# A hybrid retention, convolution and expert layer on one core: the written-out orders of four engines redone ahead of the gather stream

## The chip, the cores and the metric

The kernel runs on one core of a Trainium2 chip. The metric is the device time of one execution in microseconds. All arithmetic is float32. Five engines run their own instruction lists in parallel and meet at semaphores: PE (TensorE, matmuls and transposes), DVE (VectorE), ACT (ScalarE), POOL (GpSimd) and SP (SyncE, which here only issues DMAs). POOL also issues the indirect DMAs, called gathers below.

## What is computed

The reference runs one layer on 512 prompt frames and 32 frames of a running stream, 544 rows of 1024 numbers. Cut to what matters:

```python
h = rmsnorm(x, norm_mix)
q, k, v, g, a, b = split(h @ w_in)               # 4 x 512 for retention, 2 x 512 for the convolution
s_new, o = scan(retention_block, state, (rotary(q), rotary(k), v))   # 4 heads of 128
y_ret = silu(g) * group_norm(o)
c = depthwise_conv(concat(conv_buf, a * sigmoid(b)), taps=31) + bias
y_conv = silu(layer_norm(c))
x = x + concat(y_ret, y_conv) @ w_out
h2 = rmsnorm(x, norm_ffn)
for each of 8 heads:                             # product-key experts
    scores = two key halves of (h2 @ peer_query) against 128 keys each
    16 best sums of the two top-16 lists -> 16 experts of 16384, gate = softmax
    act = gelu(h2 . peer_down[expert]);  x = x + sum(gate * act * peer_up[expert])
return rmsnorm(x, norm_final), new states
```

## The kernel before

The 544 rows are cut in five tiles: 0 to 3 of 128 prompt rows, and tile 4 (`SAMPLE`) of 32 stream rows. The expert part is 34 "virtual tiles": head times prompt tile (32 of them), and two in which the 32 stream rows of four heads lie side by side. Each virtual tile needs 16 gathers. A gather fetches for each of 128 rows the line of one expert, `peer_down` beside `peer_up`, 8 KB a row and 1 MB in all. 544 gathers go through a ring of 12 slots in the tile `arena`. On each gathered slot DVE takes 128 dot products (`weigh`, L1329), ACT makes gelu, weight and a diagonal matrix of weights (`group`, L899 to L917), and PE adds the `peer_up` halves into PSUM by a matmul with this diagonal (`sum_up`, L1686). For the first eight gathers DVE does that sum (`sum_here`, L1339). When a slot has been used, POOL may gather into it again (`gathers`, L603).

The part ahead of the full stream is what the change touches. The same `arena` first holds the weights and the projections z = q, k, v, g of all tiles, so that the first gathers can only go out as z is used up. The steps and their names, with t the tile:

- `qkvg.s.t` (L1549, for the sample L1546): projection of section s (0 q, 1 k, 2 v, 3 g) on PE, 8 matmuls of 512 columns (16 records in the trace); ACT copies the result (`rows_in`).
- `ln_mean.b`, `ln_var.b` (L1558): channel sums of the convolution output on PE, b = 0 for the first 128 rows and 1 for the other 416. DVE subtracts the mean (`mean_off`), ACT squares (`squares`, L758) and takes the root (`root`, L763), DVE adds the squares and makes the inverse deviation (`square_sums`, `variance`, `inverse_deviation`, L1098 to L1122), then `conv_norm` (L1127, L1131), ACT `tanh`, DVE `conv_silu` (L1139). The whole convolution of 31 taps lies on DVE ahead of it and ends with L1220, which sets the semaphore `s_conv`.
- POOL turns q and k (`rotary`, L553 to L560) and weighs keys by decay (`decayed_keys`, L569).
- `head(t)` is `ret_qT.t` and `ret_kT.t`, four transposes each (L1508), copied by ACT (`turned_heads`, L735); `ret_scores.t` (L1575) and DVE's decay on it (L1151); `ret_out.t` (L1587, L1589); `ret_state.t` (L1596).
- `ret_out.t` is normed by head: DVE statistics (`ret_stats`, L1159), POOL `retention_root` (L574 to L578), ACT `head_norms` (L742), DVE times the gate (`ret_norm`, L1169), PE transposes it back (`ret_yT.t`), ACT copies (`turned_back`, L751). The gate comes from `gated` (L1078).
- `mix_out.t.i` (L1549 on `region_b`, for the sample L1546): output product, half i; DVE adds it to x (`mix_add`, L1195). ACT squares x (`mixed_squares`, L661), POOL takes the root (`mixed_root`), DVE norms (`peer_norm`, L1252), PE transposes (`ffn_t.t`), then `query.t` (L1620) and `scores.t` (L1633), copied by ACT (`first_query`, `first_scores`, L834).
- DVE searches the 16 best in three steps, `top_first`, `top_second`, `top_sums` (L1264 to L1314). The last line writes `expert`, the row numbers that the gathers of this virtual tile read.

No scheduler decides any order. PE runs through `plan()`; the other engines run through calls written out one by one, and two lists, `EMPTY_ORDER`, state in which order DVE and ACT empty the PSUM banks. PE's jobs take the eight banks in turn, and a wait is a comparison with the number of jobs done:

```python
JOB = {name: n for n, name in enumerate(JOBS)}
BANK = {name: n % BANKS if n < FIRST_SUM else ...}
def filled(name):
    act.wait_ge(s_pe, JOB[name] + 1)
```

So the engines that read a job wait for all PE jobs ahead of it too. POOL's first gathers wait for more than their expert numbers (shortened):

```python
pool.wait_ge(s_idx, 1)
gathers(0, 0, 1)
retention_root(2)
gathers(0, 2, 4)
gathers(0, 6, 10)                                  # each waits for sum_here to free its slot
pool.wait_ge(s_pe, JOB[("ret_yT", 4)] + 1)
gathers(0, 15, TOPK)
pool.wait_ge(s_pe, JOB[("mix_out", SAMPLE, 0)] + 1)
gathers(1, 0, 2)
```

Of the kernel before, what the change touches and what calls it, by code (L numbers as in the profile page):

```python
# [118 lines left out]
def plan():  # L119

    def rows(s, *tiles):
        return [("qkvg", s, t) for t in tiles]
# [4 lines left out]
    def scores(t):  # L127
        return [("ret_scores", t)]
# [68 lines left out]
ln_mean.0 ln_mean.1 ln_var.0 ln_var.1 ret_scores.0 ret_state.0 mix_out.0.0 mix_out.0.1 ret_scores.1 ret_state.1  # L197
ret_scores.2 mix_out.1.0 mix_out.1.1 ret_state.2 ret_scores.3 mix_out.2.0 ret_state.3 mix_out.2.1 ret_scores.4
mix_out.3.0 mix_out.3.1 mix_out.4.0 mix_out.4.1 ret_state.4
# [4 lines left out]
qkvg.3.1 qkvg.3.2 qkvg.3.4 ret_yT.0 ret_qT.1 ret_kT.1 qkvg.3.3 ffn_t.0.0 ffn_t.0.1 ret_qT.2 ret_kT.2 ret_out.1 query.0  # L204
scores.0 ret_yT.1 ret_out.2 ret_qT.3 ret_kT.3 ret_yT.2 ffn_t.1.0 ffn_t.1.1 ret_out.3 ret_qT.4 ret_kT.4 query.1
ret_yT.3 scores.1 ret_out.4 ret_yT.4 ffn_t.2.0 ffn_t.2.1 query.2 scores.2 ffn_t.3.0 ffn_t.3.1 ffn_t.4.0 ffn_t.4.1
# [30 lines left out]
def build(nc, x_prompt, x_sample, x_turned, state_ret, conv_state, weights, head_weights, params, consts, gain_ffn, gain_final,  # L237
          experts, y_prompt, y_sample, ret_prompt, ret_sample, conv_prompt, conv_sample):
    ctx = ExitStack()
    with ctx:  # L240
# [280 lines left out]
        def _(pool):  # L521
# [64 lines left out]
            rotary(2)  # L586
            rotary(3)
            retention_root(0)
# [32 lines left out]
            gathers(0, 2, 4)  # L621
            pool.wait_ge(s_pe, JOB[("ret_yT", 1)] + 1)
# [3 lines left out]
            mixed_root(1)  # L626
            decayed_keys(3)
# [31 lines left out]
        def _(act):  # L659
# [137 lines left out]
            turned_back(0)  # L797
            turned_heads(1)
            rows_in(S_G, 3)
# [140 lines left out]
            normalized(0)  # L940
            head_norms(2)
            turned_heads(3)
            mixed_squares(1)
            turned_back(2)
            turned_rows(1)
            group(0, 0)
            head_norms(3)
            turned_heads(4)
            first_query(1)
            turned_back(3)  # L950
            first_scores(1)
# [6 lines left out]
            turned_rows(2)  # L958
            mixed_squares(3)
            mixed_squares(SAMPLE)  # L960
            normalized(1)
            first_query(2)
            group(0, 2)
            first_scores(2)
            turned_rows(3)
            group(0, 3)
            turned_rows(4)
            group(1, 0)
            first_query(3)
# [10 lines left out]
            later_query(1, 1)  # L980
            group(2, 1)
            later_query(1, 2)
            later_query(1, 3)
            group(2, 2)
            later_scores(1)
# [31 lines left out]
        def _(dve):  # L1017
# [367 lines left out]
            gate_scales(0)  # L1385
            mix_add(1, 1)
            ret_norm(2)
            ret_state(2)
            ret_scores(3)
            dve.wait_ge(s_gain, 16)  # L1390
            peer_norm(1)
            weigh(0, 0)
            mix_add(2, 0)
            ret_stats(3)
# [429 lines left out]
```

## Time and profile before

| what | value |
|---|---|
| median of 3 runs | 1663.01 us (1662.77 to 1663.81) |
| the profiled execution, its own time | 1664.46 us |
| its span | 1662.7 us |
| busy: PE, DVE, ACT, POOL | 83%, 71%, 34%, 43% |
| moved by DMA | 608.39 MB, 570.46 of them by the gathers |
| mean granted TensorE clock | 0.946 of full speed |

A row of a timeline is: start in us from the span's start, length in us, engine, line of the kernel, operation, out<-in with shapes, x count. In brackets behind it stands how long the engine was idle before, and what released it. A row of the windows is: stretch, its length, busy us of PE, weight loads (PEld), DVE, ACT and POOL with the number of instructions, then the granted clock of PE (1.00 is 2.4 GHz, 0.50 is 1.2 GHz), the mean busy share of the 16 DMA engines, and GB/s. Matmul ends are modelled, so neighbouring rows of PE overlap by some 0.15 us.

### The profile page before, as it was taken

How to read it: one execution, taken by the hardware profiler on the slowest of the kernel's cores; microseconds unless marked ns; L12 is line 12 of the kernel's file. 1: busy time of each engine (PE TensorE's matmuls, PEld its weight loads, DVE VectorE, ACT ScalarE, POOL GpSimd, SP SyncE). 2: the span in 40 equal slices, each digit the busy share in tenths (PEclk: the TensorE clock that was granted, in tenths of full speed). 3: DMA queues.
4: the chain of work that ended last, by engine and by line, in shares of the span. 5: the costliest groups of instructions: out<-in, count | busy, mean ns of one | idle time of the engine just before them, and what ended most of it. 6: DMA issues, size and time to landing. Idle time of an engine off the chain costs nothing.

```text
span 1662.7 us, 14018 instructions
## 1 busy us (share of the span) xinstructions
PE 1383.8 (83%) x4311; PEld 678.6 (41%) x4311; DVE 1174.9 (71%) x2555; ACT 573.3 (34%) x1785; POOL 716.7 (43%) x633
## 2 busy tenths in 40 slices
PE   7999999998898789778977897789779877777733
PEld 6744465554353335324433443344324423332311
DVE  3997758966876777677767776777777777676755
ACT  3112231632433333333333333333433333333342
POOL 0004624644444445444444444445444444444552
PEclk9999999999899999999999999999999999999955
DMA  7203227999999999999999999999999999999996
GB/s 293 102 1 100 110 77 279 371 421 422 422 420 422 421 422 420 422 421 422 420 422 421 422 421 422 421 421 421 421 422 421 421 422 420 419 420 421 414 421 256
DMA packets 87978, 608.39 MB, mean 366 GB/s; under 512 B 11104, under 2 KB 13664, under 8 KB 16224
## 3 DMA queue, kind: packets, MB, share of 16 engines
q0 software_dynamic: 78336, 570.46, 82.9%
q1 hardware_dynamic: 9568, 37.04, 5.9%
q8 instruction: 34, 0.56, 0.1%
q14 instruction: 40, 0.33, 0.1%
HBM read 604.19 MB, written 2.88 MB: 365 GB/s over the span
## 4 chain that ended last, share of the span: by engine, by line
DMA 44%; PE 37%; DVE 10%; issue 3%; ACT 3%; POOL 2%; DVEq 0%; SPq 0%; POOLq 0%
DMA arena<-experts,expert 44%; PE ps L1686 18%; PE ps L1549 8%; PE ps L1649 5%; DVE arena L1329 4%; PE ps L1529 4%; POOL arena L603 2%; ACT weight L907 1%; ACT late L917 1%; PE ps L1508 1%; DVE cst L1305 0%; DVE cst L1308 0%; DVE picked L1312 0%; PE ps L1620 0%; ACT gl L899 0%
## 5 line engine op out<-in xcount | busy, mean ns | idle before, releaser
L1686 PE MATMUL ps<-arena,late 128*128 128x512 f32 x2016 | 950.3, 624 | 206.0 <-ACT late L917 205.7
L603 POOL DMA_INDIRECT arena<-experts,expert x544 | 645.2, 1186 | 732.4 <-PE ps L1686 627.5
L1329 DVE CUSTOM_DVE_ANT_0 arena<-arena,hn 128x1024 f32<-128x1024 f32 x544 | 656.7, 1222 | 384.9 <-DMA arena<-experts,expert 381.8
L1686 PEld LDWEIGHTS ps<-arena,late 128*128 128x128 f32 x2016 | 387.3, 198 | 745.0 <-issue 450.7
L899 ACT ACTIVATE gl<-dots 128x2 f32<-128x2 f32 (+1 forms) x274 | 55.8, 204 | 814.3 <-DVE dots L1329 814.3
L917 ACT ACTIVATE late<-cst,weight 128x128 f32<-128x128 f32 (+1 forms) x536 | 183.5, 389 | 8.8
L907 ACT ACTIVATE weight<-gl,gate 128x1 f32<-128x1 f32 x544 | 130.7, 287 | 8.9
L1549 PE MATMUL ps<-arena,hT 128*128 128x512 f32 x256 | 112.3, 598 | 0.0
L1649 PE MATMUL ps<-hT,region_b 128*128 128x272 f32 x448 | 106.9, 392 | 0.0
L1649 PEld LDWEIGHTS ps<-hT,region_b 128*128 128x128 f32 x448 | 85.1, 190 | 27.9 <-issue 12.4
L1072 DVE SCALAR_TENSOR_TENSOR region_b<-region_b,par 128x574 f32<-128x574 f32 x120 | 92.5, 813 | 4.5
L1549 PEld LDWEIGHTS ps<-arena,hT 128*128 128x128 f32 x256 | 48.7, 192 | 58.9 <-issue 58.8
L1680 PE MATMUL ps<-arena,late 128*32 128x256 f32 x256 | 29.7, 604 | 45.4 <-ACT late L917 45.4
L553 POOL TENSOR_TENSOR rot_tmp<-arena,cst 128x512 f32<-128x512 f32 (+1 forms) x5 | 6.3, 1265 | 124.8 <-DVE hn L1220 124.5
L1549 PE MATMUL ps<-arena,region_b 128*128 128x512 f32 x128 | 56.5, 595 | 2.5 <-issue 2.5
L1329 DVE DVE_READ_ACCUMULATOR2_ANT dots<- 128x1 f32 x544 | 44.6, 82 | 0.0
L873 ACT ACT_TABLE_LOAD x33 | 42.3, 1283 | 0.6
L899 ACT ACT_TABLE_LOAD x32 | 41.1, 1283 | 0.6
L1348 DVE TENSOR_TENSOR xs<-ps,xs 128x1024 f32<-128x1024 f32 x32 | 39.0, 1219 | 0.0
L1529 PE MATMUL ps<-hn,arena 128*128 128x272 f32 x160 | 36.8, 392 | 0.0
L1549 PEld LDWEIGHTS ps<-arena,region_b 128*128 128x128 f32 x128 | 23.8, 190 | 31.0 <-issue 30.9
L1680 PEld LDWEIGHTS ps<-arena,late 128*32 128x32 f32 x256 | 8.9, 150 | 66.1 <-ACT late L917 58.1
(174 smaller groups left out, 872.1 us busy)
## 6 DMA issues: line engine op xcount, KB each, us to landing
arena<-weights SPq DMA_DIRECT2D x6, 2048.0 KB, 11.0
region_b<-head_weights SPq DMA_DIRECT2D x8, 1152.0 KB, 9.5
arena<-experts,expert POOLq DMA_INDIRECT x544, 22.4
hT<-x_turned SPq DMA_DIRECT2D x2, 1088.0 KB, 7.2
arena<-weights SPq DMA_DIRECT2D x4, 512.0 KB, 10.7
xs<-x_prompt SPq DMA_DIRECT2D x4, 512.0 KB, 10.0
arena<-weights SPq DMA_DIRECT2D x2, 1024.0 KB, 13.9
y_prompt<-xs SPq DMA_DIRECT2D x4, 512.0 KB, 3.8
```

The source lines that it names most:

```text
L603: pool.indirect_dma_start(rows_of(n), None, experts, bass.IndirectOffsetOnAxis(ap=expert[:, vt % BUFS, k:k + 1], axis=0))\
L873: nc.scalar.activation(gate[:, u, :], best_s[:, u, :], ACT.Exp, bias=neg_max[:, u:u + 1], accum_out=gate_sum[:, u:u + 1]).then_inc(s_exp, 1)
L899: nc.scalar.activation(gl[:, vt % 2, ks], dots[:, vt % 2, ks], ACT.Gelu_apprx_tanh).then_inc(s_gelu, 1)
L907: ready = nc.scalar.activation(weight[:, vt % 2, k:k + 1], gl[:, vt % 2, k:k + 1], ACT.Copy, scale=gate[:, vt % BUFS, k:k + 1])
L917: nc.scalar.activation(diag[:, n % DIAGS, 0:base.shape[-1]], base, ACT.Copy, scale=weight[:, vt % 2, k:k + 1])\
L1072: return v.scalar_tensor_tensor(out=conv[:, c, :], in0=u[:, c, j:j + WIDE], scalar=gain, in1=conv[:, c, :], op0=ALU.mult, op1=ALU.add)
L1329: last = v.tensor_tensor_reduce(out=rows_of(n)[:, 0:D], in0=rows_of(n)[:, 0:D], in1=hn[:, tile_of(vt)], scale=1.0, scalar=0.0, op0=ALU.mul ...
L1348: v.tensor_tensor(out=xs[:, tile], in0=total, in1=xs[:, tile], op=ALU.add).then_inc(s_acc, 1)
L1529: last = mm(out[:, 0:HALF], w[:, c, k, :], columns[:, k, i * HALF:(i + 1) * HALF], start=k == 0, stop=k == KD - 1)
L1549: last = mm(out, lhs[:, k, lo:lo + r], w[:, k, :], start=k == 0, stop=k == KD - 1)
L1649: last = mm(ps[:, Q_BANKS + i, 0:HALF], weights[:, k, s * KEYS:(s + 1) * KEYS], hT[:, k, half * HALF:(half + 1) * HALF], start=k == 0, sto ...
L1686: last = mm(ps[:, 2 * (vt % 2) + half, :], diag[:, n % DIAGS, :], rows_of(n)[:, D + half * SEC:D + (half + 1) * SEC], start=k == first * G ...
```

## The change

Nothing is computed differently, and no size changes. On PE, DVE, ACT and POOL the steps named above change places, from the last k rows to virtual tile 3. SP's list is the same. The core of the diff:

```diff
@@ plan()
-    order += rows(S_Q, 2) + rows(S_K, 1) + rows(S_Q, 3) + rows(S_V, 3) + rows(S_K, 2)
-    order += [("ln_mean", 0)] + rows(S_Q, SAMPLE) + head(0) + [("ln_mean", 1), ("ln_var", 0)] + rows(S_K, 3)
-    order += [("ln_var", 1)] + scores(0) + rows(S_G, 0) + [("ret_out", 0)] + rows(S_G, 1) + [("ret_state", 0)]
-    order += rows(S_G, 2, SAMPLE) + back(0) + head(1) + rows(S_G, 3) + mix(0, 0) + mix(0, 1) + scores(1)
-    order += [("ret_out", 1)] + turn("ffn_t", 0) + [("ret_state", 1)] + head(2) + query(0) + back(1) + scores(2)
-    order += keys(0) + mix(1, 0) + [("ret_out", 2)] + mix(1, 1) + head(3) + [("ret_state", 2)] + back(2) + scores(3)
-    order += mix(2, 0) + turn("ffn_t", 1) + out(3) + head(4) + mix(2, 1) + query(1) + back(3) + scores(4) + keys(1)
-    order += mix(3, 0) + [("ret_out", 4)] + mix(3, 1) + [("ret_state", 4)] + back(4) + mix(4, 0) + mix(4, 1)
+    order += rows(S_Q, 2) + rows(S_V, 3) + rows(S_Q, 3) + rows(S_K, 1) + [("ln_mean", 0)] + rows(S_K, 2)
+    order += rows(S_Q, SAMPLE) + head(0) + [("ln_var", 0)] + [("ln_mean", 1)] + rows(S_K, 3) + scores(0)
+    order += [("ln_var", 1)] + rows(S_G, 0) + rows(S_G, 1) + [("ret_out", 0)] + rows(S_G, 2, SAMPLE)
+    order += [("ret_state", 0)] + back(0) + rows(S_G, 3) + mix(0, 0) + mix(0, 1) + head(1) + head(2) + scores(1)
+    order += [("ret_out", 1)] + turn("ffn_t", 0) + [("ret_state", 1)] + query(0) + back(1) + keys(0) + scores(2)
+    order += mix(1, 0) + [("ret_out", 2)] + mix(1, 1) + head(3) + [("ret_state", 2)] + back(2) + scores(3) + mix(2, 0)
+    order += out(3) + head(4) + turn("ffn_t", 1) + mix(2, 1) + query(1) + back(3) + keys(1) + scores(4)
+    order += [("ret_out", 4)] + mix(3, 0) + mix(3, 1) + [("ret_state", 4)] + back(4) + mix(4, 0) + mix(4, 1)
@@ gpsimd
             rotary(2)
+            retention_root(0)
             rotary(3)
-            retention_root(0)
...
             gathers(0, 2, 4)
+            decayed_keys(3)
+            mixed_root(1)
             pool.wait_ge(s_pe, JOB[("ret_yT", 1)] + 1)
             gathers(0, 4, 5)
             pool.wait_ge(s_pe, JOB[("ret_yT", 2)] + 1)
             gathers(0, 5, 6)
-            mixed_root(1)
-            decayed_keys(3)
@@ scalar
             squares(0)
             rows_in(S_Q, SAMPLE)
+            root(0)
+            squares(1)
             turned_heads(0)
-            squares(1)
-            root(0)
+            root(1)
             rows_in(S_K, 3)
-            root(1)
             rows_in(S_G, 0)
+            head_norms(0)
             tanh(0)
-            head_norms(0)
...
             turned_back(0)
+            rows_in(S_G, 3)
             turned_heads(1)
-            rows_in(S_G, 3)
...
             first_query(0)
+            turned_back(1)
             act.wait_ge(s_yconv, len(BLOCKS))
             first_scores(0)
-            turned_back(1)
@@ vector
             inverse_deviation(0)
+            ret_scores(0)
             variance(1)
-            ret_scores(0)
             inverse_deviation(1)
+            conv_norm(0)
+            conv_norm(1)
             gated(0)
             ret_stats(0)
-            conv_norm(0)
-            conv_norm(1)
             ret_norm(0)
             conv_silu(0)
+            ret_state(0)
             gated(1)
+            mix_add(0, 0)
+            gated(2)
             conv_silu(1)
-            gated(2)
-            ret_state(0)
             gated(SAMPLE)
+            mix_add(0, 1)
             gated(3)
-            mix_add(0, 0)
-            mix_add(0, 1)
             ret_scores(1)
```

The other hunks move, on DVE and ACT, the gate of virtual tile 0, head copies, dots, searches and PSUM sums of virtual tiles 0 to 3 by one or two places each, and on PE `sum_up(2, 0)` behind two of the query products of head 1. The two lists of `EMPTY_ORDER` follow these orders.

Three places show what moves. PE's list at the last k rows (L1549 is a projection, 40 or 48 matmuls are five or six of them; L1558 on `hn` is `ln_mean.0`; L1546 is the sample's q, and L1508 behind it head 0):

```order
 L1546 MATMUL ps<-arena,hT 32x128 x64
-L1549 MATMUL ps<-arena,hT 128x512 x48
+L1549 MATMUL ps<-arena,hT 128x512 x40
 L1558 MATMUL ps<-hn,ones_cw 128x128
+L1549 MATMUL ps<-arena,hT 128x512 x8
 L1546 MATMUL ps<-arena,hT 32x128 x32
 L1508 MATMUL ps<-cst,arena 128x128 x8
```

The channel mean moved ahead of the last of six projections, `qkvg.1.2`.

DVE's list behind the inverse deviation of the 416 rows (L1078 is the gate of tile 0, L1159 and L1162 are `ret_stats(0)`, L1127 and L1131 `conv_norm`, L1169 is `ret_norm(0)`), the counterpart of POOL's `retention_root(0)`, which the diff shows ahead of `rotary(3)`:

```order
-L1078 SCALAR_TENSOR_TENSOR arena<-late,arena 128x512
-L1159 BN_STATS bn<-ps 128x6 x4
-L1162 BN_AGGR mv<-bn 128x2 x4
 L1127 TENSOR_TENSOR region_b<-region_b,var 128x4x128
 L1131 TENSOR_SCALAR region_b<-region_b,half_ln 128x128 x4
 L1127 TENSOR_TENSOR region_b<-region_b,var 128x4x416
 L1131 TENSOR_SCALAR region_b<-region_b,half_ln 128x416 x4
+L1078 SCALAR_TENSOR_TENSOR arena<-late,arena 128x512
+L1159 BN_STATS bn<-ps 128x6 x4
+L1162 BN_AGGR mv<-bn 128x2 x4
 L1169 TENSOR_TENSOR hn<-hn,arena 128x512
```

The gate and the statistics of tile 0 moved behind both calls of `conv_norm`.

PE's list at the sample's retention (L1575 is `ret_scores.4`, L1633 `scores.1`, L1549 `mix_out.3.0`, L1587 with L1589 `ret_out.4`):

```order
 L1508 MATMUL ps<-cst,hn 128x128 x4
+L1633 MATMUL ps<-region_b,late 128x128 x2
 L1575 MATMUL ps<-hn 32x32 x4
-L1633 MATMUL ps<-region_b,late 128x128 x2
-L1549 MATMUL ps<-arena,region_b 128x512 x8
 L1587 MATMUL ps<-arena,hn 32x128
 L1589 MATMUL ps<-state,hn 32x128
```

The product `mix_out.3.0` no longer stands between the sample's scores and its `ret_out.4`; it comes behind.

## Rows read from the trace of the kernel before

**Rows 1.** the page: its length, and the queue of the gathers

```profile
span 1662.7 us, 14018 instructions
...
q0 software_dynamic: 78336, 570.46, 82.9%
```

**Rows 2.** windows: busy us (x instructions) by engine, PEclk, DMA share, GB/s

```profile
257.00:267.00 10.00, 10.00 (x53) 6.49 (x52) 7.64 (x18) 4.07 (x14) 5.94 (x7) 1.00 0.01 5
...
293.00:300.00 7.00, 6.26 (x141) 5.76 (x131) 5.96 (x18) 6.81 (x15) 4.71 (x6) 1.00 0.91 298
300.00:1641.00 1341.00, 1094.91 (x2884) 505.84 (x2886) 941.28 (x2154) 491.27 (x1586) 630.93 (x537) 0.94 1.01 420
```

**Rows 3.** timeline of POOL, four gathers: start, length, line, [idle before, releaser]

```profile
238.31 1.22 POOL L603 DMA_INDIRECT arena<-experts,expert  x1 [13.55 <-DVE expert L1314]
...
264.37 2.11 POOL L603 DMA_INDIRECT arena<-experts,expert  x1 [0.17 <-DVE xs L1339]
...
291.71 1.09 POOL L603 DMA_INDIRECT arena<-experts,expert  x1 [4.93 <-PE ps L1508]
...
295.14 1.34 POOL L603 DMA_INDIRECT arena<-experts,expert  x1 [0.88 <-PE ps L1546]
```

**Rows 4.** timeline of PE, K rows to the mixing products: its stalls

```profile
154.04 1.06 PE L1508 MATMUL ps<-cst,arena 128*128 128x128 f32 x8 [2.03 <-issue]
...
192.21 0.66 PE L1508 MATMUL ps<-cst,hn 128*128 128x128 f32 x4 [2.94 <-DVE hn L1169]
...
194.06 8.24 PE L1549 MATMUL ps<-arena,hT 128*128 128x512 f32 x16
...
218.01 0.49 PE L1587 MATMUL ps<-arena,hn 128*128 128x128 f32 x2 [1.09 <-DVE hn L1151]
...
230.13 7.11 PE L1549 MATMUL ps<-arena,region_b 128*128 128x512 f32 x16 [1.61 <-issue]
...
249.62 7.11 PE L1549 MATMUL ps<-arena,region_b 128*128 128x512 f32 x16 [0.63 <-issue]
...
273.24 7.11 PE L1549 MATMUL ps<-arena,region_b 128*128 128x512 f32 x16 [0.27 <-issue]
```

**Rows 5.** timeline of PE, and windows of 1 us, behind a stall of 3 us

```profile
349.06 8.83 PE L1686 MATMUL ps<-arena,late 128*128 128x512 f32 x16 [2.98 <-ACT late L917]
...
351.00:352.00 1.00, 1.00 (x3) 0.48 (x2) 0.93 (x4) 0.59 (x2) 0.00 (x0) 0.50 1.01 421
```

**Rows 6.** timeline of DVE: work beside busy POOL, and beside idle POOL (144.21)

```profile
144.21 0.76 DVE L1218 TENSOR_TENSOR hn<-region_b 128x574 f32<-128x574 f32 x1
...
173.38 1.50 DVE L1116 TENSOR_TENSOR region_b<-region_b 128x416 f32<-128x416 f32 x1
...
186.00 5.56 DVE L1131 TENSOR_SCALAR region_b<-region_b,half_ln 128x416 f32<-128x416 f32 x4
```

**Rows 7.** timeline of DVE, of ACT and of POOL

```profile
145.04 0.76 DVE L1220 TENSOR_TENSOR hn<-hn 128x574 f32<-128x574 f32 x1
...
181.03 0.88 DVE L1159 BATCH_NORM_STATS2 bn<-ps 128x6 f32<-128x128 f32 x4
...
191.48 0.68 DVE L1169 TENSOR_TENSOR hn<-hn,arena 128x512 f32<-128x512 f32 x1
...
150.96 0.63 ACT L758 ACTIVATE region_b<-region_b 128x512 f32<-128x512 f32 x1 [0.42 <-DVE region_b L1090]
...
186.08 1.51 ACT L742 ACTIVATE hn<-ps,rstd,ret_rstd 128x128 f32<-128x128 f32 x4 [1.29 <-POOL rstd L578]
...
221.87 0.23 POOL L574 TENSOR_SCALAR rstd<-mv 128x4 f32<-128x4 f32 x1 [3.02 <-DVE mv L1162]
...
223.56 0.20 POOL L578 TENSOR_TENSOR rstd<-rstd,ret_rstd 128x4 f32<-128x4 f32 x1
```

**Rows 8.** timeline of DVE: sums of tile 0, and dots behind gather 7

```profile
261.45 5.44 DVE L1339 SCALAR_TENSOR_TENSOR xs<-arena,weight,xs 128x1024 f32<-128x1024 f32 x4
...
274.62 1.22 DVE L1329 CUSTOM_DVE_ANT_0 arena<-arena,hn 128x1024 f32<-128x1024 f32 x1 [2.50 <-DMA arena<-experts,expert]
```

More of the change, by code:

```diff
@@ L196 @@
 EMPTY_ORDER = {"dve": named("""
-ln_mean.0 ln_mean.1 ln_var.0 ln_var.1 ret_scores.0 ret_state.0 mix_out.0.0 mix_out.0.1 ret_scores.1 ret_state.1
+ln_mean.0 ln_mean.1 ln_var.0 ret_scores.0 ln_var.1 ret_state.0 mix_out.0.0 mix_out.0.1 ret_scores.1 ret_state.1
 ret_scores.2 mix_out.1.0 mix_out.1.1 ret_state.2 ret_scores.3 mix_out.2.0 ret_state.3 mix_out.2.1 ret_scores.4
-mix_out.3.0 mix_out.3.1 mix_out.4.0 mix_out.4.1 ret_state.4
+mix_out.3.0 mix_out.3.1 mix_out.4.0 ret_state.4 mix_out.4.1
 """), "act": named("""
@@ L203 @@
 qkvg.1.4 qkvg.1.0 qkvg.0.2 qkvg.1.1 qkvg.0.3 qkvg.2.3 qkvg.1.2 qkvg.0.4 ret_qT.0 ret_kT.0 qkvg.1.3 qkvg.3.0 ret_out.0
-qkvg.3.1 qkvg.3.2 qkvg.3.4 ret_yT.0 ret_qT.1 ret_kT.1 qkvg.3.3 ffn_t.0.0 ffn_t.0.1 ret_qT.2 ret_kT.2 ret_out.1 query.0
-scores.0 ret_yT.1 ret_out.2 ret_qT.3 ret_kT.3 ret_yT.2 ffn_t.1.0 ffn_t.1.1 ret_out.3 ret_qT.4 ret_kT.4 query.1
-ret_yT.3 scores.1 ret_out.4 ret_yT.4 ffn_t.2.0 ffn_t.2.1 query.2 scores.2 ffn_t.3.0 ffn_t.3.1 ffn_t.4.0 ffn_t.4.1
+qkvg.3.1 qkvg.3.2 qkvg.3.4 ret_yT.0 qkvg.3.3 ret_qT.1 ret_kT.1 ffn_t.0.0 ffn_t.0.1 ret_qT.2 ret_kT.2 ret_out.1 query.0
+ret_yT.1 scores.0 ret_out.2 ret_qT.3 ret_kT.3 ret_yT.2 ret_qT.4 ret_kT.4 ffn_t.1.0 ffn_t.1.1 ret_out.3 query.1
+scores.1 ret_yT.3 ret_out.4 ret_yT.4 ffn_t.2.0 ffn_t.2.1 query.2 scores.2 ffn_t.3.0 ffn_t.3.1 ffn_t.4.0 ffn_t.4.1
 query.3 scores.3 scores.4
@@ L934, in _ @@
             first_query(0)
+            turned_back(1)
             act.wait_ge(s_yconv, len(BLOCKS))
             first_scores(0)
-            turned_back(1)
             softmax(0)
             gelu_next()
-            normalized(0)
             head_norms(2)
             turned_heads(3)
+            turned_back(2)
             mixed_squares(1)
-            turned_back(2)
+            turned_heads(4)
+            normalized(0)
+            group(0, 0)
             turned_rows(1)
-            group(0, 0)
             head_norms(3)
-            turned_heads(4)
             first_query(1)
+            first_scores(1)
             turned_back(3)
-            first_scores(1)
             group(0, 1)
@@ L958, in _ @@
             turned_rows(2)
+            normalized(1)
             mixed_squares(3)
             mixed_squares(SAMPLE)
-            normalized(1)
+            group(0, 2)
             first_query(2)
-            group(0, 2)
             first_scores(2)
+            group(0, 3)
             turned_rows(3)
-            group(0, 3)
+            group(1, 0)
             turned_rows(4)
-            group(1, 0)
-            first_query(3)
             softmax(2)
@@ L972, in _ @@
             normalized(2)
+            first_query(3)
             group(1, 2)
@@ L980, in _ @@
             later_query(1, 1)
+            later_query(1, 2)
             group(2, 1)
-            later_query(1, 2)
             later_query(1, 3)
+            later_scores(1)
             group(2, 2)
-            later_scores(1)
             normalized(3)
@@ L1385, in _ @@
             gate_scales(0)
+            ret_norm(2)
             mix_add(1, 1)
-            ret_norm(2)
             ret_state(2)
             ret_scores(3)
+            weigh(0, 0)
             dve.wait_ge(s_gain, 16)
             peer_norm(1)
-            weigh(0, 0)
+            ret_stats(3)
             mix_add(2, 0)
-            ret_stats(3)
             ret_state(3)
@@ L1402, in _ @@
             sum_here(1)
+            mix_add(3, 0)
             ret_stats(SAMPLE)
             top_second(1)
-            mix_add(3, 0)
             ret_norm(SAMPLE)
@@ L1408, in _ @@
             mix_add(3, 1)
+            mix_add(SAMPLE, 0)
+            gate_scales(1)
             peer_norm(2)
-            mix_add(SAMPLE, 0)
+            ret_state(SAMPLE)
             mix_add(SAMPLE, 1)
-            gate_scales(1)
-            ret_state(SAMPLE)
             weigh(0, 2)
@@ L1417, in _ @@
             weigh(0, 3)
+            weigh(1, 0)
             top_first(2)
-            weigh(1, 0)
             top_second(2)
             top_sums(2)
-            add(0)
+            gate_scales(2)
             weigh(1, 1)
-            gate_scales(2)
             weigh(1, 2)
             top_first(3)
+            add(0)
             top_second(3)
+            top_sums(3)
             weigh(1, 3)
-            top_sums(3)
             weigh(2, 0)
             gate_scales(3)
-            add(1)
             weigh(2, 1)
             weigh(2, 2)
-            weigh(2, 3)
+            add(1)
             top_first(4)
-            weigh(3, 0)
             top_second(4)
             top_sums(4)
+            weigh(2, 3)
+            weigh(3, 0)
             weigh(3, 1)
@@ L1442, in _ @@
             top_first(5)
+            top_second(5)
+            top_sums(5)
             weigh(3, 2)
-            top_second(5)
             weigh(3, 3)
-            top_sums(5)
             for vt in range(4, VT - 2):
@@ L1737, in _ @@
                     sum_up(step[1], step[2])
+            sum_up(2, 0)
             later_query(1, 0)
             later_query(1, 1)
-            sum_up(2, 0)
             later_query(1, 2)
```

## Prediction

> **What bounds the kernel now.** Read the page first, its length and its queues [rows 1]: one queue, the gathers, moves 570 MB in a span of 1662.7 us and takes 82.9% of all 16 DMA engines' time. Then the windows [rows 2]. They say when the stream is full for good: from 300 to 1641 us the DMA share is 1.01 at 420 GB/s, and before that it has a hole from 257 to 267 (share 0.01) and is short again from 293 to 300 (0.91). So 1341 us of the span are bytes over a rate, and an order of instructions changes neither. What an order can change is when the stream becomes unbroken. The timeline of POOL [rows 3] names what each gather waited for. The first (238.31) waited for the expert numbers from VectorE, the seventh (264.37) for a weighted sum that frees a slot, the sixteenth (291.71) for a transpose on PE (`ret_yT.4`), the seventeenth (295.14) for the product `mix_out.4.0` on PE. From the sixteenth on the queue is never empty long enough to matter. Hence the rule for this change: the end moves by as much as gathers 15 and 16 (numbered from 0) move, and these hang on the end of PE's list before the full stream. An earlier first gather alone only makes the hole behind it wider.
>
> PE does the same matmuls before and after, so its end moves by the difference of its stalls and slow stretches. The timeline of PE [rows 4] has those of before between the last K rows and `mix_out.3.1`: 2.03, 2.94, 1.09, 1.61, 0.63 and 0.27 us, together 8.6. One product took 8.24 instead of 7.11 us behind the stall of 2.94 (1.1 more). Smaller pieces, without a row, I put at 0.6. Sum 10.3 us.
>
> **The change, part by part.**
>
> *Mean before K rows.* `ln_mean.0` now stands ahead of `qkvg.1.2`. It needs the channel sum that VectorE ends at 145.04 + 0.76 = 145.8 [rows 7]. PE gets there at 142.9: head 0 came at 154.04 after a stall of 2.03 [rows 4], so PE was done at 152.0, and the sample product and one product of 7 us lie ahead of that. PE now stalls 2.9 us, and the stall of 2.03 goes. A stall of that length lowers the granted clock in this trace: behind 2.98 us idle the window at 351 shows 0.50 (1.2 GHz), and the 16 records took 8.83 us where 7.11 is usual [rows 5, 4]. Price 1.7 us; bounds 0 (behind 2.03 us nothing slowed) and 1.7; I take 1.7, as 2.9 is nearer to 2.98. ScalarE's `squares(0)` still stands behind the copy of those K rows, so it leaves 150.96 [rows 7] for about 155.5: the early mean brings nothing, and `ln_var.0`, which PE now asks for ahead of `ln_mean.1`, comes 0.9 us late.
>
> *VectorE without POOL.* `retention_root(0)` moves ahead of `rotary(3)` on POOL, and on VectorE `ret_stats(0)`, which it waits for, moves behind both `conv_norm`. POOL's list thus stops at about 171.8, with `rotary(2)`, until `ret_stats(0)`. Queued behind it are `rotary(3)`, `rotary(4)`, `decayed_keys(1)`; the first needs them at `ret_kT.3` near 242 and ends near 205, so nobody waits. VectorE then works alone. Beside a busy POOL a 416-column operation took 1.50 us and four of them 5.56; beside an idle POOL one of 574 columns took 0.76 [rows 6]. So 416 columns alone cost 0.6 (estimate by columns), bounds 0.6 and 1.5. Four such in `inverse_deviation(1)` and four in `conv_norm(1)` save 8 x 0.9 = 7.2 us. The reciprocal of the same width I leave as it is, since no row shows it shorter. Against it: the late squares, and the root ahead of `squares(1)`, cost the chain 4 us. And three things now follow `conv_norm(1)` in a row: the statistics (0.88, and some 0.3 for their sums), POOL's root (221.87 to 223.76, 1.9) and `head_norms(0)` (1.5) [rows 7], together 4.6 us, of which the statistics' 1.2 lay on the chain before too. The gate of tile 0, beside an idle POOL, takes 0.9 less. `ret_norm(0)` ended at 192.2 [rows 7] and comes at 192.2 - 7.2 + 4 + 4.6 - 1.2 - 0.9 = 191.5. PE, with K rows late and both G products ahead of `ret_out.0`, asks for it at 192.5, 1 us later. The stall of 2.94 goes, and the 1.1 of slow clock with it.
>
> The Trainium skill ("SBUF — State Buffer", Who interferes with whom) says that VectorE and GpSimd share one port pair as an exclusive lock, that two SBUF inputs or a 2-port mode need it, and that other one-input operations do not. By this rule the multiplications shorten and the reciprocal does not, as in the sum; rows 6 agree (1.50 against 0.76).
>
> *Heads 1 and 2 behind the mixing products.* 1.8 us of transposes move; no work is added. `mix_out.0.1` then ends about 2 us earlier. `ret_out.1` still waits for `ret_scores(1)`: 0.6 in place of 1.09. Head 2 no longer stands between the rows of tile 0 and `query.0`. ScalarE has `turned_back(1)` ahead of `first_scores(0)`, so `mix_out.1.0` does not wait (1.61 goes), while the search gets its scores 1 us later than it could. The first gather goes out about 1.9 us earlier, at 236.4. Ahead of `mix_out.2.0` 0.2 in place of 0.63.
>
> *`ret_out.4` ahead of `mix_out.3.0`.* It needs `ret_scores(4)`, which VectorE has behind `weigh(0, 1)`, and that waited 2.50 us for gather 7 until 274.62 [rows 8]. Gather 6 leaves when the sum of tile 0 (261.45, rows 8) has freed its slot; head 4 and the sums come 4.5 us earlier, and the POOL piece behind them too, so gather 6 goes out 5.4 us earlier (264.37 to about 259) and gather 7 lands at 269.2. `weigh(0, 1)` and `ret_scores(4)` end at 270.9, PE is there at 268.8: a new stall of 2.0, where the product of 7 us covered it before. The 0.27 goes.
>
> The sum of stalls after: 2.9 + 1.7 + 0.9 + 0.6 + 0.2 + 2.0 = 8.3 us against 10.3: PE ends its list **2.0 us** earlier, gathers 15 and 16 go out at 289.7 and 293.1, and the stream becomes whole 2.0 us sooner. Behind it nothing counts: dots, searches, sums and projections of tiles 1 to 3 change places under a queue that is full [rows 2]. The profiled execution took 1664.46 us for a span of 1662.7, 1.45 above the median of 1663.01; less 2.0 it is 1662.5, and the median 1661.0. A measurement of this kernel tells about 0.2% (3.3 us) from no change.
>
> **The rivals.** (a) *The clock holds.* If PE keeps 2.4 GHz through the stall of 2.9, as it did through 2.03, and the stall at `ret_out.4` is gone because gather 7 lands in time, it is 1661.0 - 1.7 = 1659.3 for the first and 1657.3 for both. For it: 2.9 is at the edge. Against: rows 5, and the same happened behind 2.94.
> (b) *The clock falls twice.* The new stall of 2.0 to 2.5 follows the small matmuls of scores 1 and head 4; with 1.7 more it is 1662.7. For it: a stall of 2.94 behind such small work was enough [rows 4]. The Trainium skill ("TensorE: Matmul & The Clock Gate", Part 4) holds that transposes do not count as busy in the way that matmuls do, which speaks for it, as this stretch has them; rows 4 have 2.03 us idle with no slow product behind, which speaks against.
> (c) *Slower: VectorE is not freed.* If the 1.50 us is the operation's own length, `ret_norm(0)` comes 7.2 us later, at 198.7. It decides from 192.5 on, when PE wants it: PE stalls 6.2 us before `ret_yT.0`, and the clock falls once more (1.7). 1661.0 + 6.2 + 1.7 = 1668.9. For it: no row shows a 416-column operation beside an idle POOL. Against: 574 columns in 0.76.
> (d) *The stream ignores it.* If gathers 15 and 16 had slack the end would stay at 1663.0. Against: the queue was short of work just there (share 0.91 from 293 to 300, rows 2).
>
> **How the numbers follow.** Forecast 0.38; (a) 0.34; (b) and (d) 0.12; (c) 0.11; the rest 0.05. The range 1656.5 to 1666.0 holds the forecast, (a), (b), (d) and part of the way to (c); the forecast's own is 1659.5 to 1662.5. Faster than 1659.7 is (a) with the forecast's lower edge, 0.37; slower than 1666.3 is (c) and some of the rest, 0.13; within 0.2% 0.50.
>
> **What would show it.** Step one: PE idle near 143 for 3 us, PEclk at 0.5 behind it, `squares(0)` near 155. Step two: no POOL row between 172 and 186, 416-column rows near 0.6 us, no stall before `ret_yT.0`. Step three: first gather near 236.4, `mix_out.1.0` without a stall. Step four: PE waiting for VectorE's `ret_scores(4)` near 269 for about 2 us. The end: gathers 15 and 16 near 289.7 and 293.1. It is wrong if the span moves otherwise than these two do, or if the DMA share falls below 1 anywhere between 300 and 1641.

## The result, and the profile after

| what | before | the change |
|---|---|---|
| median | 1663.55 us (14 runs) | 1667.22 us (14 runs, 1666.29 to 1670.88) |
| ratio | | 1.0025, 95% interval 1.0016 to 1.0033 |
| the profiled execution, its span | 1664.46, 1662.7 us | 1667.13, 1665.3 us |
| mean granted TensorE clock | 0.946 | 0.944 |

The change is slower, by 3.7 us. The forecast was 1661.0, and its range ended at 1666.0. A sentence of the section on the change has to be read the right way round: on PE, `sum_up(2, 0)` moves from *behind* the first two query products of head 1 to *ahead* of them, so that all four products now stand in one row, with `sum_up(2, 1)` behind them.

The windows of after, with the columns of [rows 2], and four stretches more. The rows at 273, 288, 388 and 394 were not shown of before: there the clock is 1.00 in all four, and the shares at 288, 388 and 394 are 1.00, 1.01 and 1.00.

```profile
257.00:267.00 10.00, 10.00 (x45) 6.17 (x45) 9.05 (x14) 3.96 (x14) 7.20 (x9) 1.00 0.59 214
273.00:274.00 1.00, 1.00 (x5) 0.36 (x4) 1.00 (x2) 0.00 (x0) 0.00 (x0) 0.50 0.99 418
...
288.00:293.00 5.00, 4.69 (x17) 2.24 (x15) 4.73 (x15) 0.27 (x2) 0.02 (x1) 1.00 0.10 41
293.00:300.00 7.00, 4.99 (x136) 4.32 (x136) 5.00 (x17) 5.98 (x15) 4.78 (x6) 1.00 0.71 226
300.00:1641.00 1341.00, 1097.16 (x2892) 509.77 (x2892) 940.94 (x2154) 491.24 (x1585) 641.65 (x538) 0.94 1.01 420
...
388.00:394.00 6.00, 6.00 (x15) 2.66 (x14) 0.00 (x0) 0.00 (x0) 2.82 (x3) 1.00 0.76 277
394.00:400.00 6.00, 4.53 (x26) 3.26 (x25) 3.83 (x18) 4.04 (x14) 0.94 (x1) 1.00 0.98 367
```

The hole from 257 to 267 is half filled, as gather 6 goes out earlier. A new one stands from 288 to 293, and one more at 388, inside the stream that [rows 2] showed as full. The long window hides it: two or three us in 1341 round away in a share of 1.01. That is the first thing to learn here, since the forecast rested on that long window.

POOL of after, the same gathers as [rows 3]: the first, number 6, 15 and 16, then the two on either side of the hole at 388.

```profile
237.46 1.22 POOL L603 DMA_INDIRECT arena<-experts,expert  x1 [13.48 <-DVE expert L1314]
...
259.65 2.06 POOL L603 DMA_INDIRECT arena<-experts,expert  x1 [0.22 <-DVE xs L1339]
...
292.98 1.06 POOL L603 DMA_INDIRECT arena<-experts,expert  x1 [5.78 <-PE ps L1508]
...
296.42 1.02 POOL L603 DMA_INDIRECT arena<-experts,expert  x1 [0.89 <-PE ps L1546]
...
373.08 1.14 POOL L603 DMA_INDIRECT arena<-experts,expert  x1 [0.78 <-PE ps L1686]
389.96 0.94 POOL L603 DMA_INDIRECT arena<-experts,expert  x1 [15.74 <-PE ps L1686]
```

PE of after, its timeline at the places of [rows 4]: the channel sums, the transposes of tile 0, the mixing products of tiles 1 and 2, the retention output of the stream rows and what follows it, and the sums behind the searches that [rows 5] showed.

```profile
146.37 0.79 PE L1558 MATMUL ps<-hn,ones_cw 128*128 128x128 f32 x2 [2.81 <-DVE hn L1220]
...
192.52 0.60 PE L1508 MATMUL ps<-cst,hn 128*128 128x128 f32 x4
...
271.54 0.40 PE L1587 MATMUL ps<-arena,hn 32*32 32x128 f32 x2 [1.59 <-DVE hn L1151]
...
273.09 0.63 PE L1587 MATMUL ps<-arena,hn 32*32 32x128 f32 x2
...
275.35 16.00 PE L1549 MATMUL ps<-arena,region_b 128*128 128x512 f32 x32
...
356.34 16.46 PE L1686 MATMUL ps<-arena,late 128*128 128x512 f32 x32 [6.04 <-ACT late L917]
372.64 14.83 PE L1649 MATMUL ps<-hT,region_b 128*128 128x272 f32 x64
387.31 7.03 PE L1686 MATMUL ps<-arena,late 128*128 128x512 f32 x16
```

VectorE of before, then of after, at the first dot product of `weigh(1, 3)`:

```profile
345.45 1.22 DVE L1329 CUSTOM_DVE_ANT_0 arena<-arena,hn 128x1024 f32<-128x1024 f32 x1
```

```profile
352.74 1.22 DVE L1329 CUSTOM_DVE_ANT_0 arena<-arena,hn 128x1024 f32<-128x1024 f32 x1
```

So there are two losses, and they are read in this order. **At 271.54** PE waits 1.59 us, and from 272.6 to 279.4 it runs at half clock (the window at 273 shows 0.50): the small products of `ret_out.4` take 3.8 us in place of 2.67, and the 32 mixing records 16.00 in place of 13.9, together 3.2 us. Gather 15 goes out at 292.98, 1.3 us *later* than before. **At 356.34** PE waits 6.04 us for scaled copies where it waited 2.98 [rows 5], because VectorE's dots `weigh(1, 3)` begin at 352.74 and not at 345.45. The sums that free the slot for the gather at 389.96 (number 48) start at 387.31, not at 379.26; before, that gather left at 381.92. The last packet of the gather ahead of it ended at 390.3 before and ends at 391.5 after. So before the queue still had 8.4 us of work when this gather was issued, and after it has 1.6: the queue runs dry.

The DMA packets say what each costs. The table gives, in us against before, when the last packet of a gather of queue 0 ended (gathers numbered from 0; 144 packets each, in the order in which they ended), for this profile and for those of the experiments below.

| gather | change | kernel 1 | kernel 2 | kernel 3 | kernel 4 | kernel 7 | kernel 8 |
|---|---|---|---|---|---|---|---|
| 15 | +1.6 | +0.8 | +0.9 | -2.2 | -1.8 | -1.6 | -5.6 |
| 30 | +0.2 | -0.3 | +2.1 | -2.4 | -2.5 | -2.3 | -6.1 |
| 46 | +0.3 | -0.3 | +2.1 | -2.4 | -2.6 | -2.3 | -6.1 |
| 96 | +2.9 | -0.3 | +5.0 | +2.2 | -2.6 | +1.7 | -6.1 |
| 528 | +2.4 | -0.4 | +4.8 | +1.8 | -2.2 | +1.3 | -6.0 |

Between 46 and 96 lies the dry stretch, 2.7 to 4.7 us where there is one. In kernels 2, 3 and 7 it has a second, shorter part: from 412 to 420 their shares are 0.94, 0.94 and 0.92, where the change and kernel 4 have 1.02 and 1.00.

Between 15 and 30 a profile can gain or lose a us or more by itself. Kernel 2 has PE's code of before up to there and shows +2.1. Its PE at `mix_out.4.0`, below that of before:

```profile
292.38 3.76 PE L1546 MATMUL ps<-arena,region_b 128*32 128x128 f32 x128 [0.96 <-issue]
```

```profile
292.75 5.37 PE L1546 MATMUL ps<-arena,region_b 128*32 128x128 f32 x128 [0.96 <-issue]
```

Behind the same wait of 0.96 us the clock fell in one profile (0.50 from 293 to 296) and held in the other (1.00). So one profile can't give the price of the start of the stream; for that the medians of the runs are used.

### The profile page after: what moved, and what is told of

Read it like the earlier page. It is cut to its first block, busy times and chain, and to the rows that moved or that the text cites. A ratio compares the mean times of both kernels' runs of the same rounds, so it can differ in the third digit from the quotient of the medians.

```text
span 1665.3 us, 14018 instructions
## 1 busy us (share of the span) xinstructions
PE 1388.1 (83%) x4311; PEld 682.0 (41%) x4311; DVE 1163.4 (70%) x2555; ACT 571.3 (34%) x1785; POOL 724.4 (43%) x633
## 4 chain that ended last, share of the span: by engine, by line
DMA 41%; PE 35%; DVE 13%; issue 4%; DVEq 3%; ACT 2%; POOL 2%; SPq 0%; POOLq 0%; ACTq 0%
DMA arena<-experts,expert 41%; PE ps L1686 20%; PE ps L1549 6%; PE ps L1649 5%; DVE arena L1329 4%; DVE region_b L1072 3%; DVEq L1213 3%; PE ps L1529 2%; POOL arena L603 2%; ACT weight L907 1%; ACT late L917 1%; DVE cst L1305 1%; DVE cst L1308 1%; DVE picked L1312 1%; DVE best_i L1271 0%
## 5 line engine op out<-in xcount | busy, mean ns | idle before, releaser
L603 POOL DMA_INDIRECT arena<-experts,expert x544 | 657.3, 1208 | 722.2 <-PE ps L1686 606.3
L1549 PE MATMUL ps<-arena,hT 128*128 128x512 f32 x256 | 112.5, 598 | 0.0
L1549 PEld LDWEIGHTS ps<-arena,hT 128*128 128x128 f32 x256 | 49.0, 193 | 59.7 <-issue 59.4
L1549 PE MATMUL ps<-arena,region_b 128*128 128x512 f32 x128 | 58.2, 611 | 0.4 <-issue 0.4
L1549 PEld LDWEIGHTS ps<-arena,region_b 128*128 128x128 f32 x128 | 24.7, 197 | 30.5 <-issue 30.4
```

Of the source, the lines that this page charges most:

```text
L603: pool.indirect_dma_start(rows_of(n), None, experts, bass.IndirectOffsetOnAxis(ap=expert[:, vt % BUFS, k:k + 1], axis=0))\
L1549: last = mm(out, lhs[:, k, lo:lo + r], w[:, k, :], start=k == 0, stop=k == KD - 1)
```

## The experiments

Two theories stood at first. Theory E: the early stall and clock fall at `ret_out.4` cost the time. Theory L: the late order does, through the dry stretch. Each kernel ran 11 or 12 times beside 33 or 35 runs of before. The interval of a ratio is 0.0009 to either side, which is 1.5 us; a difference of two medians is no surer than that. The kernels are numbered as they ran.

**1. The late part undone.** The change, with this taken back (VectorE's dots and searches from `weigh(1, 0)` on, two ScalarE copies and PE's sums):

```diff
-            top_first(3)
-            add(0)
-            top_second(3)
-            top_sums(3)
-            weigh(1, 3)
+            add(0)
...
+            top_first(3)
+            top_second(3)
+            weigh(1, 3)
+            top_sums(3)
...
-            sum_up(2, 0)
             later_query(1, 0)
             later_query(1, 1)
+            sum_up(2, 0)
```

> The changed kernel with the late part of the change alone undone (TensorE: sums (2,0) again between the first and the last two query products of head 1; ScalarE: the scaled copies (2,1) and (2,2) again ahead of a query copy and the score copies; VectorE: dots and searches of tiles 1 to 3 in the old order). Theory L (the late order lets the full stream run dry once near 390 us): about 3 us faster than the change, 1664.2 us, and no hole in the transfers near 388 to 400 us. Theory E (the stall and the second clock fall near 270 us, which delay gathers 15 and 16 by 1.3 us, cost the time): 1667.2 us, within 0.5 of the change.

Measured: 1665.56 us, ratio 1.0012 (1.0003 to 1.002), 1.7 us better than the change (2.2 by the ratios). The share from 388 to 394 is 1.02. The hole is gone, but not all of the loss: the time lies between what theories L and E had.

**2. The late part alone**, the same hunks put into the kernel before.

> The kernel before with only that late part of the change put in. Theory L: about 3 us slower than before, 1666.5 us, with a hole in the transfers near 385 to 400 us though everything up to 330 us is as before. Theory E: 1663.5 us, as before.

Measured: 1666.85 us, ratio 1.0019 (1.001 to 1.0028): 3.2 us slower than before, with 15.95 us of idle POOL ahead of the same gather and a share of 0.93 from 388 to 394. The late part by itself makes a slow kernel. That settles theory L as one half. The profile's own time, 1669.68 us, is 2.8 above the median and has the clock fall at 293 in it.

**3. The retention output back behind its cover.**

```diff
-    order += [("ret_out", 4)] + mix(3, 0) + mix(3, 1) + [("ret_state", 4)] + back(4) + mix(4, 0) + mix(4, 1)
+    order += mix(3, 0) + [("ret_out", 4)] + mix(3, 1) + [("ret_state", 4)] + back(4) + mix(4, 0) + mix(4, 1)
```

> The changed kernel with the retention output of the sample tile behind the first half of mix 3 on TensorE again, all else as in the change. Both theories expect no stall near 270 us and no second clock fall, and gathers 15 and 16 some 3 us earlier (near 290 and 293 us). Theory E: the time falls by 1.3 to 3.3 us, to 1664 to 1666. Theory L: the stream is held at its dry stretch near 390 us, which stays where it was, so 1667.2 us, within 0.7.

Measured: 1665.06 us, ratio 1.0006 (0.9997 to 1.0014), 2.2 us better than the change (3.2 by the ratios). PE and POOL of this kernel:

```profile
271.23 7.11 PE L1549 MATMUL ps<-arena,region_b 128*128 128x512 f32 x16 [1.18 <-issue]
278.27 0.40 PE L1587 MATMUL ps<-arena,hn 32*32 32x128 f32 x2
...
289.70 1.06 POOL L603 DMA_INDIRECT arena<-experts,expert  x1 [6.58 <-PE ps L1508]
293.13 1.02 POOL L603 DMA_INDIRECT arena<-experts,expert  x1 [0.89 <-PE ps L1546]
```

No clock fall, and gathers 15 and 16 at 289.70 and 293.13: what the forecast had, 289.7 and 293.1. But the table shows that of the 2.4 us that the stream is ahead at gather 46 nothing is left at gather 96 (this profile, 1666.39 us, is 1.3 above the kernel's median). Theory L had no gain here and was off by 2 us; theory E had 1664 to 1666, which holds. Both hold in part, so they were joined.

**4. Both undone.**

> Both undone at once: the retention output of the sample tile behind the first half of mix 3, and the late part in the old order. Theory L: 1664.2 us if the start of the full stream is absorbed by the slack near 312 to 320 us as in the kernel before, down to 1660.9 if it is not (gathers 15 and 16 then come 1.9 us earlier than before the change). Theory E alone: as the third kernel of this call, 1664 to 1666.

Measured: 1662.09 us, ratio 0.9986 (0.9978 to 0.9995). 5.1 us better than the change, a little more than the two gains apart (1.7 and 2.2). That would fit one limit hiding behind the other, but the excess is within the uncertainty. With these two places mended the rest of the change is a gain of 1.5 us on before (2.3 by the ratio), near the 2.0 of the forecast.

**5 to 7. Which piece of the late part?** Kernel 4, with one engine's piece put back in each time: PE's, ScalarE's, VectorE's.

> The fourth kernel (retention output and late part undone) with TensorE's piece of the late part alone put back in: sums (2,0) ahead of all four query products. Theory V (VectorE's searches ahead of the dots (1,3) start the dry stretch): 1662.1 us, as the fourth kernel, within 0.7. Theory P (14.8 us of query products in one row let the ring run dry): 3 us slower than the fourth, 1665 us, with a hole near 390 us. Theory J (no piece alone delays the sums (2,1) past the 7 us or so that the queue has in hand; it takes all three): 1662.1 us.

> The fourth kernel with ScalarE's piece alone put back in: the copy of the third query piece ahead of the scaled copies (2,1), the score copies ahead of (2,2). All theories: sums (2,1) begin about 1 us later than at 377.1 us, since the scaled copies wait for the third query product. Theories V, P and J: 1662.1 us within 0.7. Were it ScalarE alone that dries the ring: 1665 us.

> The fourth kernel with VectorE's piece alone put back in: searches of tiles 3 to 5 ahead of the last dots. All theories: TensorE idle 6 us instead of 1.4 ahead of the sums (1,3), which then begin near 355 us instead of 348.6. Theory V: the stream runs dry near 390 us, 3 us slower than the fourth, 1665 us. Theory J: the delay of 6 to 7 us is just what the queue has in hand, 1662.1 to 1663 us. Theory P: 1662.1 us.

Measured: PE's 1662.04 us, ratio 0.9993 (0.9984 to 1.0002); ScalarE's 1662.11, ratio 0.999 (0.9981 to 0.9999); VectorE's 1665.93, ratio 1.0011 (1.0002 to 1.002). It is VectorE's piece, alone, by 3.8 us against kernel 4. Theories P (PE's four products in a row do it) and J (it takes all three pieces) fall. PE of kernel 4, then of kernel 7, at the same place:

```profile
348.57 7.13 PE L1686 MATMUL ps<-arena,late 128*128 128x512 f32 x16 [1.35 <-ACT late L917]
355.55 7.50 PE L1649 MATMUL ps<-hT,region_b 128*128 128x272 f32 x32
362.88 7.03 PE L1686 MATMUL ps<-arena,late 128*128 128x512 f32 x16
369.75 7.50 PE L1649 MATMUL ps<-hT,region_b 128*128 128x272 f32 x32
377.08 7.03 PE L1686 MATMUL ps<-arena,late 128*128 128x512 f32 x16
```

```profile
353.63 9.36 PE L1686 MATMUL ps<-arena,late 128*128 128x512 f32 x16 [6.33 <-ACT late L917]
...
384.36 7.03 PE L1686 MATMUL ps<-arena,late 128*128 128x512 f32 x16
```

POOL of kernel 4, then of kernel 7, at gather 48:

```profile
379.73 1.44 POOL L603 DMA_INDIRECT arena<-experts,expert  x1 [8.49 <-PE ps L1686]
```

```profile
387.02 0.94 POOL L603 DMA_INDIRECT arena<-experts,expert  x1 [8.04 <-PE ps L1686]
```

The sums that free slots begin 7.3 us later: 5.1 from the wait, the rest from the slow clock behind it (9.36 us in place of 7.13). The wait comes from VectorE, which has `add(0)` and `top_sums(3)` ahead of the dots instead of behind them: 1.1 and 5.2 us in its timeline. These two are read from the timeline and were not put back one by one. The piece also moves the searches of tiles 4 and 5 against later dots, and gather 56 goes out at 410.29 in place of 395.96, which goes with the second dip at 412.

The last packet of the gather ahead of number 48 ended at 387.7 in kernel 4 and 388.9 in kernel 7. So the queue had 8.0 us in hand in kernel 4, the delay was 7.3, and 1.9 us were left in kernel 7. That is too little, for two reasons that the traces show. A gather's first packet comes behind its issue, by 1.75 us for gather 15 of the change (292.98 to 294.73). And the 16 DMA engines don't run out together: the share of kernel 7 is down to 0.76 from 386 to 388, before the last packet. Over all the kernels, those with 5.0 us or more in hand at this gather (before, 1, 4, 5, 6, 8, 9, 11, 12) have shares of 1.00 to 1.02 from 388 to 394; those with 1.6 to 2.7 (the change, 2, 3, 7, 10) have 0.76 to 0.93.

**9. The same, inside the change**, with VectorE's piece alone undone.

> The changed kernel with VectorE's piece of the late part alone undone; TensorE's and ScalarE's pieces, the retention output and the channel sums stay as in the change. If the dots (1,3) behind the searches are what dries the stream: as the first kernel, about 1665.6 us, and no hole near 390 us. If TensorE's and ScalarE's pieces need only a later stream to bite: nearer 1667.2.

Measured: 1666.0 us, ratio 1.0008 (0.9999 to 1.0017), and a share of 1.02 from 388 to 394. As kernel 1, within 0.5. PE's four products in a row stay in it (14.83 us, then sums at 383.48), and they do no harm: 5.2 us are still in hand at gather 48.

**8. The channel sums back.** Kernel 4, with

```diff
-    order += rows(S_Q, 2) + rows(S_V, 3) + rows(S_Q, 3) + rows(S_K, 1) + [("ln_mean", 0)] + rows(S_K, 2)
+    order += rows(S_Q, 2) + rows(S_V, 3) + rows(S_Q, 3) + rows(S_K, 1) + rows(S_K, 2) + [("ln_mean", 0)]
```

> The fourth kernel with the first channel sums (ln_mean.0) behind the third key product again, so that TensorE doesn't wait 2.8 us there. The clock should not fall at 147 us (or fall later, as it did before the change near 154 us at a stall of 2.0 us). If the early stall and fall count: all from there on comes up to 1.7 us earlier, gather 6 near 258 and gather 15 near 288 us, and the time is 1660.4 us. If the two slow periods only change places: 1662.1 us.

Measured: 1659.13 us, ratio 0.9978 (0.9969 to 0.9987): the fastest kernel, 3.7 us under before by the ratio. PE:

```profile
150.13 0.38 PE L1558 MATMUL ps<-hn,ones_cw 128*128 128x128 f32 x2
150.44 1.96 PE L1546 MATMUL ps<-arena,hT 128*32 128x128 f32 x64
154.41 1.06 PE L1508 MATMUL ps<-cst,arena 128*128 128x128 f32 x8 [2.01 <-issue]
```

A stall of 2.01 stands in place of one of 2.80 with a clock fall behind it. Gather 15 goes out at 286.27, 3.4 us earlier than in kernel 4, and the median is 3.0 us lower, below the 1660.4 expected. That fits a start of the stream that counts us for us where nothing behind it is dry; but by the ratios it is only 1.3 us, so the medians can't prove the factor.

**10. The channel sums back in the change itself**, with its two losses left in.

> The changed kernel with the first channel sums alone behind the third key product again. Expected: no stall and no fall at 147 us, TensorE 3.4 us ahead from there, the stall before the retention output at 270 us and its clock fall stay (gather 7 comes 3.4 us earlier too). If what bounds the end is the start of the stream: 1664 us. If the dots (1,3) bound it: they are counted from the landing of gathers that also come 3.4 us earlier, so again about 1664; only a bound that does not move with the start (1667) would speak against the picture.

Measured: 1664.44 us, ratio 1.0005 (0.9995 to 1.0014), 2.8 us better than the change. As expected: the dry stretch moves with the start. The stall at `ret_out.4` is 1.25 us here, and the clock falls behind it all the same.

**11 and 12. POOL beside VectorE.** Kernel 8, first with POOL's piece undone, then with VectorE's `conv_norm` behind `ret_stats(0)` again too:

```diff
             rotary(2)
-            retention_root(0)
             rotary(3)
+            retention_root(0)
```

> The eighth kernel (fastest so far) with POOL's third rotary step ahead of its root of tile 0 again, VectorE's order as in the change. If two engines slow each other: POOL is busy from 172 to 181 us, the 416-column operations of the inverse deviation take 1.5 us instead of 0.6 (about 3.6 us more), the normalization of tile 0 comes 3 us later, TensorE waits for it at 189 us, and the time is 1661 to 1663 us. If not: as the eighth, 1659.1.

> The same with VectorE's normalizations of the convolution behind gate and statistics of tile 0 again too, so that POOL and VectorE work side by side from 172 to 196 us as before the change. If contention is the price: 416 columns take 1.5 us and four scalings 5.6 us, the normalization of tile 0 comes about 3 to 4 us later than in the eighth, TensorE stalls about that long, and the time is 1661 to 1664 us. If VectorE's own order is what counts: slower by the statistics' place only, under 1 us.

Measured: 1665.07 us, ratio 1.0005 (0.9996 to 1.0014), and 1664.7 us, ratio 0.9997 (0.9988 to 1.0006). VectorE in kernel 8 and then in kernel 11, with only POOL's order between them; the operations at 174.32 and 175.00 are alike in size, as those at 175.65 and 176.57:

```profile
171.49 2.75 DVE L1114 RECIPROCAL region_b<-region_b 128x416 f32<-128x416 f32 x1 [0.62 <-ACT region_b L763]
174.32 0.59 DVE L1116 TENSOR_TENSOR region_b<-region_b 128x416 f32<-128x416 f32 x1
...
175.65 0.38 DVE L1120 TENSOR_SCALAR region_b<-region_b 128x416 f32<-128x416 f32 x1
...
187.71 1.39 DVE L1169 TENSOR_TENSOR hn<-hn,arena 128x512 f32<-128x512 f32 x1 [3.61 <-ACT hn L742]
```

```profile
171.19 2.75 DVE L1114 RECIPROCAL region_b<-region_b 128x416 f32<-128x416 f32 x1 [0.61 <-ACT region_b L763]
...
175.00 1.50 DVE L1118 TENSOR_TENSOR region_b<-region_b,var 128x416 f32<-128x416 f32 x1
176.57 1.28 DVE L1120 TENSOR_SCALAR region_b<-region_b 128x416 f32<-128x416 f32 x1
...
191.41 1.35 DVE L1169 TENSOR_TENSOR hn<-hn,arena 128x512 f32<-128x512 f32 x1 [3.61 <-ACT hn L742]
```

Contention is the price: with POOL busy until 181 us, four of VectorE's operations (L1118 to L1127) are 0.9 to 1.0 us longer each and the one ahead of them 0.3, and the normalization of tile 0 comes 3.7 us later. PE of kernel 11, then of kernel 12:

```profile
192.81 0.66 PE L1508 MATMUL ps<-cst,hn 128*128 128x128 f32 x4 [3.75 <-DVE hn L1169]
193.30 8.73 PE L1549 MATMUL ps<-arena,hT 128*128 128x512 f32 x16
```

```profile
193.11 0.66 PE L1508 MATMUL ps<-cst,hn 128*128 128x128 f32 x4 [3.22 <-DVE hn L1169]
193.60 7.03 PE L1549 MATMUL ps<-arena,hT 128*128 128x512 f32 x16
```

In kernel 11 the clock falls too, gather 15 goes out at 291.64 (5.4 us later than in kernel 8) and the median is 5.9 us higher, above the 1661 to 1663 expected, which had no clock fall. In kernel 12 it doesn't fall; gather 15 is at 290.22, 4.0 us later than in kernel 8. Its median, 5.6 us up and above the 1661 to 1664 expected, is more than that, its ratio (0.9997 against 0.9978, 3.2 us) a little less. The times of these two kernels lie in two groups each: five from 1661.36 to 1662.98 and six from 1664.70 to 1665.50 in kernel 12, six from 1658.09 to 1659.13 and five from 1661.19 to 1662.29 in kernel 8. The median of kernel 12 falls in its upper group and that of kernel 8 in its lower one. Group against group it is 3.8 and 3.6 us, close to the 4.0 of gather 15. What parts the groups isn't shown. A clock fall that comes in some executions only, as at 293 in kernel 2, is a candidate, but that one made its product only 1.6 us longer. In either way of reading this part of the change was worth 3 to 6 us.

## Why the prediction was wrong

- **Mean before K rows: right.** Stall 2.81 us (2.9 said), half clock behind it, `squares(0)` at 155.89 (155.5). It was rightly counted as a loss, of 2.6 us in the sum: moving it back brings gather 15 3.4 us earlier and the median 3.0.
- **VectorE without POOL: right.** POOL is idle 14.73 us up to 186.90, the multiplications of 416 columns take 0.59 us and four scalings 1.72, the reciprocal stays at 2.75, `ret_norm(0)` ends at 191.8 (191.5 said) and PE does not wait at 192.52. By the Trainium skill ("SBUF — State Buffer", Who interferes with whom) it is the shared port pair that VectorE's operations wait for; the trace agrees, with 1.50 and 0.59 us for two inputs and 2.75 both ways for the reciprocal. Rival (c) is refuted, and kernels 11 and 12 show what it would have cost.
- **Heads 1 and 2 behind the mixing products: right in kind.** `mix_out.1.0` did not wait. The first gather went out at 237.46 (236.4 said), 0.9 us earlier than before and not 1.9; nothing in the sum hung on it.
- **`ret_out.4` ahead of `mix_out.3.0`: the stall was right (1.59, said 2.0), the clock was not in the sum.** This is rival (b), and its term of 1.7 us measured 3.2: the clock was low for 6.8 us, not for about 3.4. Without it the sum holds to a tenth (292.98 less 3.2 is 289.8, and 289.7 was said), with some luck: the 0.9 ahead of `ln_var.0` measured 0.26, and a wait of 0.56 ahead of `ret_yT.1` was not in it. So the start of the stream moved +1.3 us, not -2.0.
- **"Behind it nothing counts: dots, searches, sums and projections of tiles 1 to 3 change places under a queue that is full": the step that failed.** It is worth 3.2 us on the kernel before, 3.8 in kernel 7, and 1.7 when it is undone in the change. It was argued from a window of 1341 us and from the DMA share alone. What it needed was the reserve: how long the last gather already issued still runs when the next one is issued. The last section of the prediction named the sign (a share below 1 between 300 and 1641), but no term was worked out for it, though [rows 5] held half of the answer: PE was already waiting 2.98 us for those very copies.
- The sum, by the profile: the start 1.3 us later and the dry stretch 2.7, together 4.0, where the medians have 3.7. The kernels of the experiments divide it otherwise: 2.0 us remain with the late part undone (kernel 1), and 1.7 go with it. Both divisions are within the 1.5 us, so that two causes are shown, but not the exact share of each.

What stays open: the window from 300 to 312 has a granted clock of 0.86 in the change and in kernels 1 to 4, where before has 1.00. In the change PE waits 2.62 us there for ScalarE's `first_query(2)`, which now stands behind `group(0, 2)`, where it waited 0.47 before. But kernel 2 has the old order and waits of 0.47 and 1.27 there, and its clock falls too. The order of first queries and scaled copies was not tried apart. Nor does anything here say why the clock falls in one profile and holds in another behind the same wait.

## What to carry to other kernels

A resource whose share is 1.0 over a long stretch is safe only as far as its reserve goes: for each step that frees a buffer, compare how much later it comes with what the queue still has in hand (here 8.0 us, of which some 3 to 5 must be left when the next gather is issued), in windows no longer than that. On an engine that feeds such a queue, put the work that frees buffers (dots, sums) ahead of work for later tiles (searches), and give a wait for another engine a long product as cover, above all behind small matmuls, where here a wait of 1.59 us brought 6.8 us of half clock. Reordering for a neighbour's sake pays too: beside an idle POOL VectorE's products of 416 columns took 0.59 us in place of 1.50, though its reciprocal gained nothing.

## What the runs showed of the hardware

- How long PE was idle does not say by itself whether the clock falls. It fell behind 1.23 us (kernel 1), 1.25 (kernel 10), 1.59 (the change) and 2.26 (kernel 9), each time with small matmuls before and the 32-row products of `ret_out.4` behind; with `mix_out.3.0` behind, at the same place, it did not fall at 1.18 us (kernels 3 and 4). It did not fall at 2.01 (kernel 8) or 3.22 (kernel 12), and it did at 2.81 (the change) and 3.75 (kernel 11). Behind 0.96 us ahead of `mix_out.4.0` it fell in the profile of kernel 2 and held in that of before, with the same matmuls around it.
- A fall's length differs: 6.8 us at 0.50 behind 1.59 us idle, but about 3.4 behind 2.81 (both in the change).
- A queue of gathers loses share before its last packet is done. With 5.0 us in hand at the next issue (kernel 5) its share stayed at 1.01, with 1.9 (kernel 7) it fell to 0.76 and 0.67 in the two stretches of 2 us from 386.
- A one-input operation profits from an idle POOL as well: the scaling of 416 columns took 1.28 us beside a busy POOL (kernel 11) and 0.38 beside an idle one (kernel 8).
